# The odd mixer's input projection in seven block products instead of eight

## The reference, cut to what matters

```
def odd_mixer(h, cos, sin, cos_i, sin_i, w_in, w_out):
    qc, kc, vc, qi, ki, wi, qd, kd, vd = split_cols(h @ w_in, ODD_SPLITS)
    c_out = dsa_attention(partial_rope(qc...), partial_rope(kc...), vc, partial_rope(qi...), partial_rope(ki...), wi)
    d_out = moba_attention(partial_rope(qd...), partial_rope(kd...), vd)
    return jnp.concatenate([c_out, d_out], axis=-1) @ w_out
```

## Time and profile before

| | before |
|---|---|
| median of 3 runs | 3152.28 us (3148.3 to 3156.09) |
| the profiled execution, device time | 3152.17 us |
| its span in the trace | 3150.0 us |
| mean granted TensorE clock | 0.994 |
| TensorE matmuls busy | 3076.6 us (98%) |
| VectorE busy | 1917.6 us (61%) |
| ScalarE busy | 788.5 us (25%) |
| DMA, mean over the span | 211 GB/s |

### The profile page before, as it was taken

One profiled execution on the slowest core, in us unless ns is written; L12 is line 12 of the kernel. 1 busy time (PEld: TensorE's weight loads), 2 busy tenths in 40 slices (PEclk: granted clock), 3 DMA queues, 4 the chain that ended last, 5 costly groups with the idle time before them and its releaser, 6 DMA issues. The chain is left out here.

```text
span 3150.0 us, 46742 instructions
## 1 busy us (share of the span) xinstructions
PE 3076.6 (98%) x18521; PEld 1797.1 (57%) x18521; DVE 1917.6 (61%) x3306; ACT 788.5 (25%) x2066; POOL 162.0 (5%) x145
## 2 busy tenths in 40 slices
PE   9999999999999999999999899999999999999998
PEld 7845686784468567775685576864433333333333
DVE  7743786775477545623575546442377776677776
ACT  4412453351245243222252234230200000000000
POOL 0000000000000002310000104110100000000000
PEclk9999999999999999999999999999999999999999
DMA  7542045354424440123444421133699999999993
GB/s 292 189 179 107 33 182 209 125 187 156 167 88 178 169 182 27 67 93 137 175 177 184 154 98 66 55 141 124 259 402 420 418 419 420 366 414 418 419 417 137
DMA packets 81046, 665.52 MB, mean 211 GB/s; under 512 B 10528, under 2 KB 11168, under 8 KB 14016
## 3 DMA queue, kind: packets, MB, share of 16 engines
q1 hardware_dynamic: 78816, 655.41, 52.7%
q10 hardware_dynamic: 2016, 7.13, 0.6%
HBM read 661.46 MB, written 1.05 MB: 210 GB/s over the span
## 5 line engine op out<-in xcount | busy, mean ns | idle before, releaser
L4231 PE MATMUL psum<-ring,arena 128*32 128x512 f32 x5376 | 582.3, 592 | 0.0
L4231 PEld LDWEIGHTS psum<-ring,arena 128*32 128x32 f32 x5376 | 178.5, 110 | 397.6 <-issue 396.7
L887 PE MATMUL psum<-ring,arena 128*128 128x256 f32 x1760 | 398.1, 379 | 0.0
L887 PEld LDWEIGHTS psum<-ring,arena 128*128 128x128 f32 x1760 | 334.2, 190 | 46.1 <-issue 0.6
L887 PE MATMUL psum<-ring,xT_norm 128*128 128x256 f32 x1320 | 305.2, 381 | 1.4 <-DMA ring<-in_ffn_w 1.4
L940 ACT ACTIVATE arena<-arena 32x128 f32<-32x128 f32 x880 | 269.7, 306 | 31.4 <-DVE arena L1074 21.8
L999 DVE TENSOR_TENSOR ring<-ring 128x1024 f32<-128x1024 f32 x220 | 267.0, 1214 | 9.7 <-DMA ring<-in_ffn_w 3.3
L887 PEld LDWEIGHTS psum<-ring,xT_norm 128*128 128x128 f32 x1320 | 251.9, 191 | 36.3 <-DMA ring<-in_ffn_w 1.8
L4381 ACT ACTIVATE arena<-psum 128x256 f32<-128x256 f32 x84 | 32.5, 387 | 782.7 <-PE psum L4231 782.7
L907 PE MATMUL psum<-ring,arena 128*128 128x512 f32 x440 | 205.8, 592 | 0.0
L3091 PE MATMUL psum<-xT_norm,ring 128*128 128x256 f32 x832 | 184.8, 381 | 0.0
(11 more groups left out here) (636 smaller groups left out, 3884.5 us busy)
## 6 DMA issues: line engine op xcount, KB each, us to landing
ring<-in_moe_w SPq DMA_DIRECT2D x340, 1024.0 KB, 9.4
ring<-in_ffn_w SPq DMA_DIRECT2D x50, 2048.0 KB, 7.8
ring<-in_ffn_w SPq DMA_DIRECT2D x65, 1024.0 KB, 4.9
ring<-in_merge_w SPq DMA_DIRECT2D x16, 2048.0 KB, 8.3
ring<-in_feat_w SPq DMA_DIRECT2D x12, 2048.0 KB, 8.7
ring<-in_ev_in_w SPq DMA_DIRECT2D x4, 2048.0 KB, 8.9
ring<-in_od_in_w SPq DMA_DIRECT2D x4, 2048.0 KB, 9.6
ring<-in_merge_w SPq DMA_DIRECT2D x8, 1024.0 KB, 11.5
```

Source lines behind the costliest of these rows:

```text
L887: last = pe.matmul(psum[:, bank, 0:GROUP], a[:, k, :], w[:, k, :], start=(fresh and k == 0), stop=(k == KT // 2 - 1), skip_group_check=True)
L4231: last = pe.matmul(psum[part(j), r, :], xg[:, u.i, u.group // GROUPS, r * P + BLOCK * j:r * P + BLOCK * (j + 1)], m[:, j, :], start=(u.i = ...
```

## The change

The product of each chunk is done by Strassen's scheme in Winograd's form. The input is cut in 2 x 2 blocks (two row blocks, two halves of the features: 11, 12, 21, 22) and the chunk's weights too (two halves of the features, two halves of the columns). Seven block products of four matmuls each, 128 rows by half a chunk's columns, take the place of 2 x 8 matmuls over the whole chunk width. VectorE makes four differences or sums of weight blocks for each chunk (T1 to T4, 128 x 1024 each, `sum_on_vector`), four of input blocks once (S1 to S4, 128 x 512 each, `mix_on_vector`), and puts the block results together from the banks (`post`: u2, v, c22, c21, c12, and c11 in chunk 0). ScalarE copies P1 out of its bank (`copy_p1`) and scales each of the four blocks of a result (`settle`). Results are complete in the order c22, c11, c21, c12.

The order on VectorE is rewritten: posts and sums stand between the entry, the rotations and the picking of keys. The rotation of qd stands ahead of the posts of chunk 2; `pick_keys(0)` between the posts of chunks 2 and 3; the rotation of kd and `pick_keys(1)` between the posts of chunks 3 and 4; the rotation of qc behind all posts of chunk 4. P4 shares a PSUM bank with P6 and waits for `u2` of its own chunk, and P3 shares one with P5 and waits for `c22`. SyncE starts the later loads when a chunk's seven products are done. The filler matmuls no longer wait for ScalarE's last emptying.

```
+CHUNK_BANK = {"P1": 0, "P2": 0, "P6": 1, "P5": 2, "P3": 2, "P7": 3, "P4": 1}
+CHUNK_POSTED = (None, "u2", "v", "c22", "c21", "c12")
...
+    def posted_at(self, c, name):
+        return 1 if name == "c11" else 5 * c + 1 + CHUNK_POSTED.index(name)
...
+    def bank(self, c, name):
+        n, h = CHUNK_BANK[name], self.half(c)
+        if c == 0 and name == "P2":
+            n = 4
+        return self.prog.psum[:, n, 0:h]
...
+    def on_tensor(self, pe, c, name):
+        left, right = BLOCK_FACTORS[name]
+        if name == "P1":
+            self.weights.wait(pe, c)
+            if c == 1:
+                pe.wait_ge(self.posted, self.posted_at(0, "u2"))
+            if c:
+                pe.wait_ge(self.settled, 4 * (c - 1) + 2)
+        elif name == "P6" and c:
+            pe.wait_ge(self.posted, self.posted_at(c - 1, "c21"))
+        elif name == "P5" and c:
+            pe.wait_ge(self.posted, self.posted_at(c - 1, "c12"))
+        elif name == "P7" and c:
+            pe.wait_ge(self.posted, self.posted_at(c - 1, "v"))
+        elif name == "P4":
+            pe.wait_ge(self.posted, self.posted_at(c, "u2"))
+        elif name == "P2" and c:
+            pe.wait_ge(self.p1_copied, c + 1)
+        elif name == "P3":
+            pe.wait_ge(self.posted, self.posted_at(c, "c22"))
+        if left[0] == "S":
+            pe.wait_ge(self.mixed, {"S1": 1, "S2": 2, "S3": 3, "S4": 4}[left])
+        if right[0] == "T":
+            pe.wait_ge(self.summed, 4 * c + int(right[1]))
+        fresh = name != "P3" and not (name == "P2" and c)
+        a, w = self.x[left], self.factor(c, right)
+        for k in range(KT // 2):
+            last = pe.matmul(self.bank(c, name), a[:, k, :], w[:, k, :], start=(fresh and k == 0), stop=(k == KT // 2 - 1),
+                             skip_group_check=True)
+        last.then_inc(self.made, 1)
+    def copy_p1(self, act, c):
+        act.wait_ge(self.made, self.made_at(c, "P1"))
+        if c:
+            act.wait_ge(self.posted, self.posted_at(c - 1, "u2"))
+        act.activation(self.temps(c)[0][:, 0:self.half(c)], self.bank(c, "P1"), ACT.Copy).then_inc(self.p1_copied, 1)
+
+    def settle(self, act, c, name, func=ACT.Copy):
+
+        b, n = {"c22": (1, 1), "c11": (0, 0), "c21": (1, 0), "c12": (0, 1)}[name]
+        to = of = self.block(c, b, n)
+        if name == "c11" and c:
+            act.wait_ge(self.made, self.made_at(c, "P2"))
+            of = self.bank(c, "P1")
+        else:
+            act.wait_ge(self.posted, self.posted_at(c, name))
+        act.activation(to, of, func, scale=self.prog.rstd[:, b:b + 1]).then_inc(self.settled, 1)
+
+    def mix_on_vector(self, dve, i):
+        out, a, b, op = (("S1", "21", "22", ALU.add), ("S2", "S1", "11", ALU.subtract),
+                         ("S3", "11", "21", ALU.subtract), ("S4", "12", "S2", ALU.subtract))[i]
+        if i in (1, 3):
+            dve.wait_ge(self.mixed, i)
+        dve.tensor_tensor(self.x[out], self.x[a], self.x[b], op).then_inc(self.mixed, 1)
+
+    def sum_on_vector(self, dve, c, i):
+        out, a, b = (("T1", "12", "11"), ("T2", "22", "T1"), ("T3", "22", "12"), ("T4", "T2", "21"))[i]
+        if i == 0:
+            self.weights.wait(dve, c)
+        elif i in (1, 3):
+            dve.wait_ge(self.summed, 4 * c + i)
+        if c and i != 2:
+            dve.wait_ge(self.made, self.made_at(c - 1, ("P5", "P6", None, "P4")[i]))
+        dve.tensor_tensor(self.factor(c, out), self.factor(c, a), self.factor(c, b), ALU.subtract).then_inc(self.summed, 1)
...
+    def post(self, dve, c, name):
+
+        h = self.half(c)
+        p1, u2, v = (t[:, 0:h] for t in self.temps(c))
+        if name == "u2":
+            dve.wait_ge(self.made, self.made_at(c, "P6"))
+            dve.wait_ge(self.p1_copied, c + 1)
+            last = dve.tensor_tensor(u2, p1, self.bank(c, "P6"), ALU.add)
+        elif name == "v":
+            dve.wait_ge(self.made, self.made_at(c, "P7"))
+            dve.wait_ge(self.posted, self.posted_at(c, "u2"))
+            last = dve.tensor_tensor(v, self.bank(c, "P7"), u2, ALU.add)
+        elif name == "c22":
+            dve.wait_ge(self.made, self.made_at(c, "P5"))
+            dve.wait_ge(self.posted, self.posted_at(c, "v"))
+            last = dve.tensor_tensor(self.block(c, 1, 1), self.bank(c, "P5"), v, ALU.add)
+        elif name == "c11":
+            dve.wait_ge(self.made, self.made_at(c, "P2"))
+            dve.wait_ge(self.p1_copied, 1)
+            last = dve.tensor_tensor(self.block(c, 0, 0), self.bank(c, "P2"), p1, ALU.add)
+        elif name == "c21":
+            dve.wait_ge(self.made, self.made_at(c, "P4"))
+            last = dve.tensor_tensor(self.block(c, 1, 0), v, self.bank(c, "P4"), ALU.subtract)
+        else:
+            dve.wait_ge(self.made, self.made_at(c, "P3"))
+            last = dve.tensor_tensor(self.block(c, 0, 1), u2, self.bank(c, "P3"), ALU.add)
+        last.then_inc(self.posted, 1)
...
         @ph.block.sync
         def _(sp):
             for i in w_in.missing():
                 if i >= 4:
-                    sp.wait_ge(bank_full, TB * (i - 3))
+                    sp.wait_ge(blocks_of.made, 7 * (i - 3))
                 w_in.start(sp, i)
-            sp.wait_ge(bank_full, TB * 4)
+            sp.wait_ge(blocks_of.made, 7 * 4)
             w_out.start(sp, 1)
-            sp.wait_ge(bank_full, TB * 5)
+            sp.wait_ge(blocks_of.made, 7 * 5)
             w_out.start(sp, 0)
             for i in range(3):
...
             def chunk(c):
-                w_in.wait(pe, c)
-                n = ODD_CHUNKS[c]
-                w = w_in.buffer(c).rearrange("p (k n) -> p k n", k=KT)
-                for tb in range(TB):
-                    if c == 2:
-                        pe.wait_ge((z_ready, z_vector)[tb], 1)
-                    elif c > 2:
-                        pe.wait_ge(z_ready, 2 * (c - 2) + tb)
-                    for k in range(KT):
-                        if c == 0 and tb == 1 and k % 4 == 0:
-                            entry.wait_block(pe, (1, k // 4))
-                        last = pe.matmul(proj(c, tb), prog.xT[:, k, tb * P:(tb + 1) * P], w[:, k, :],
-                                         start=(k == 0), stop=(k == KT - 1))
-                    last.then_inc(bank_full, 1)
+                for name in blocks_of.order(c):
+                    blocks_of.on_tensor(pe, c, name)
...
-            pe.wait_ge(z_ready, 8)
-            stay_busy(prog, pe, 2, 4)
+            stay_busy(prog, pe, 3, 4)
...
             entry.on_scalar(act)
+            blocks_of.copy_p1(act, 0)
             act.wait_ge(entry.ready, 1)
-            empty(0, 0)
-            empty(1, 0)
-            empty(1, 1)
+            settle(0, "c22", "c11", "c21", "c12")
+            blocks_of.copy_p1(act, 1)
+            settle(1, "c22", "c11", "c21", "c12")
             fill(0)
-            empty(2, 0)
-            empty(2, 1)
+            blocks_of.copy_p1(act, 2)
+            settle(2, "c22", "c11", "c21")
             rectify(0)
             rectify(1)
-            empty(3, 0)
-            empty(3, 1)
-            empty(4, 0)
-            empty(4, 1)
+            settle(2, "c12")
+            blocks_of.copy_p1(act, 3)
+            settle(3, "c22", "c11", "c21", "c12")
+            blocks_of.copy_p1(act, 4)
+            settle(4, "c22", "c11", "c21", "c12")
             for f in (2, 4, 6):
...
-            entry.on_vector(dve)
-            entry.mean_on_vector(dve)
-            entry.invert_on_vector(dve)
-            dve.wait_ge(entry.ready, 1)
-            dve.wait_ge(bank_full, 2)
-            dve.tensor_scalar(z[:, 1, 0:starts[1]], proj(0, 1), prog.rstd[:, 1:2], None, ALU.mult).then_inc(z_vector, 1)
-            dve.wait_ge(z_ready, 1)
-            dve.wait_ge(z_vector, 1)
-            turn_angles(1, QI, NI, ID, 8, 4)
-            turn_angles(2, KI, 1, ID, 8, 4)
-            turn_angles(3, KC, 1, HD, 0, 8)
-            fill(1)
-            for b in range(TB):
+            def pick_keys(b):
...
-            for c, at in ((1, QD), (2, KD), (3, QC)):
-                dve.wait_ge(z_ready, 2 * c + 1)
-                turn_angles(3 + c, at, NH, HD, 0, 8)
+            def sums_behind(c, *which):
+                for i in which:
+                    blocks_of.sum_on_vector(dve, c, i)
+
+            post = lambda c, *names: [blocks_of.post(dve, c, name) for name in names]
+
+            blocks_of.sum_on_vector(dve, 0, 0)
+            entry.on_vector(dve)
+            dve.wait_ge(entry.copied, len(entry.blocks))
+            blocks_of.mix_on_vector(dve, 0)
+            blocks_of.sum_on_vector(dve, 0, 1)
+            blocks_of.mix_on_vector(dve, 1)
+            entry.mean_on_vector(dve)
+            blocks_of.mix_on_vector(dve, 2)
+            blocks_of.sum_on_vector(dve, 0, 2)
+            entry.invert_on_vector(dve)
+            blocks_of.sum_on_vector(dve, 0, 3)
+            blocks_of.mix_on_vector(dve, 3)
+            post(0, "c11", "u2")
+            sums_behind(1, 0, 1)
```

(82 more changed lines are left out.)

## The result

The changed kernel takes 3157.56 us (median of 22 runs, 3155.26 to 3163.22) against 3152.12 us (22 runs, 3148.3 to 3157.49): 5.4 us more. The ratio is 1.0014 with a 95% interval of 1.0009 to 1.002; it is taken over all runs and isn't the quotient of the two medians (1.0017), and by it the loss is 4.4 us, 2.8 to 6.3. That is slower, and clearly so, but by less than the 0.3% that the forecast took as the limit. Its profiled execution took 3156.61 us with a span of 3154.2, mean granted clock 0.993.

A forecast was written before the change was run, and what follows sets the result against it. TensorE was taken to set the pace, until VectorE has no slack from P4 of chunk 2. Chunk 0 +2.7, chunks 1 and 2 -1.5 and -1.7, then +6.4 to chunk 4's end, tail +0.8: +6.7, 3159.0 us, range 3154.5 to 3165.

The forecast's parts named there:

- a chunk of 512 columns by seven products: TensorE, chunks 1 to 4: 56 records of 256 columns take 12.08 us for 13.79, saving 1.71 us each.
- chunk 0 on TensorE: First chunk of the odd mixer: held back by VectorE's sums and posts, it ends 2.7 us later than before.
- VectorE's entry to the last mix: VectorE at the start of the odd mixer: copies, four sums, four mixes and small steps take 6.8 us.
- wait of P4 in chunk 4: TensorE in the last chunk: P4 waits 7.5 us for u2, which stands behind the second picking on VectorE.
- P4's start, from the entry's transposes: Last chunk: P4 starts when u2 is done at 848.9, forecast as 66.7 us after the entry's transposes.
- loss of clock in P4 and P3: Behind the wait in chunk 4: half clock for 4.5 us costs these two products 2.25 us.
- tail, more than before: After chunk 4: VectorE's c12 post, late rotation of qc and three copies add 0.8 us.
- stage, more than before: From the entry's transposes to the first attention matmul: 6.7 us longer, the whole forecast loss.
- first rival: Clock falls twice, also in chunk 0: end at 3161.3 us, above 3161.8 if it stays low longer; chance 0.27.
- VectorE's run: From P4 of chunk 2 on, 32 us without slack; rival: hand-overs lengthen some 35 steps, 3162 us, chance 0.08.
- The picking: Rival: second picking of keys hidden, so TensorE doesn't wait in chunk 4; 3149.2 us, chance 0.06.
- The estimate for a 584-wide sum: VectorE in chunk 0: each of four sums takes 0.75 us, against 1.2 for a 1024-wide one.

The follow-up runs named there:

- e5: Changed kernel with chunk 0 back to 16 plain matmuls, both banks emptied on ScalarE, without VectorE's sums and posts for it; 3155.8 us, 1.0009 of the kernel before.
- r_after_1: The changed kernel profiled again, nothing altered; whole time 3157.11 us, 77.89 us from the entry's transposes to the first attention matmul.
- r_after_2: A further profiled execution of the changed kernel, nothing altered; whole time 3157.62 us, 76.58 us from the entry's transposes to the first attention matmul.
- e1: Changed kernel with only the post u2 of chunk 4 put ahead of the second picking of keys on VectorE; 3157.2 us, 1.0014 of the kernel before.
- e4: Changed kernel with seven of the eight rounds of the second picking left out; 3148.5 us, 0.9986 of the kernel before.
- e3: Changed kernel with 30 filler matmuls put where TensorE waits in chunk 4, order kept; 3150.06 us, 0.9992 of the kernel before.
- e2: Changed kernel with the second picking cut up and chunk 4's posts set between its parts; 3156.27 us, 1.0013 of the kernel before.
- e6: Changed kernel with seven products for chunks 1 and 2 alone, chunks 0, 3 and 4 plain; 3147.79 us, 0.9985 of the kernel before.
- e7: Changed kernel with seven products for chunks 1 to 3, chunks 0 and 4 plain; 3148.11 us, 0.9992 of the kernel before.

## Why the prediction was right

The forecast was 3159.0 with 0.64 on a difference under 0.3%; 3157.56 came. Its steps, each as a difference within its own execution:

| step | forecast | measured |
|---|---|---|
| a chunk of 512 columns by seven products | 12.08 us | 12.09 |
| chunk 0 on TensorE | 10.7, loss 2.7 | 10.43, loss 2.4, or 2.6 against e5's 7.86 |
| VectorE's entry to the last mix | 6.8 | 6.7 (780.06 to 786.78) |
| wait of P4 in chunk 4 | 7.5 | 7.39 |
| P4's start, from the entry's transposes | 66.7 | 66.50 |
| loss of clock in P4 and P3 | 2.25 | 3.15; 2.99 in r_after_1, 1.70 in r_after_2 |
| tail, more than before | 0.8 | 4.97 - 4.06 = 0.9 |
| stage, more than before | 6.7 | 7.5 in the profile, 7.3 and 6.0 in the others |
| attention | 0 | -1.4, or 0 |

The mechanism was right in place, and in size but for the clock: e1 shows that the wait follows the posts, e4 that it is the picking's length, e5 that chunk 0 and the wait are separate costs, e3 that the clock is one of its own. The term that was mis-sized is the clock: 2.25 us forecast, 3.15, 2.99 and 1.70 measured. "Run at half clock for 4.5 us" rested on one stretch; here it was half until 852.8, 6.2 us of work. And the forecast let the attention phase alone, which came out 1.4 us shorter. The two errors have opposite signs: 6.7 + 0.8 - 1.4 = 6.1 us, which is the 106.56 - 100.52 = 6.0 of the profiles. That they cancel is luck, and a part of why the median came so near. The 0.7 us between 6.1 and the measured 5.4 is less than the runs scatter. The 0.33 for slower by over 0.3% was too much even by the prediction's own figures, since the main case of its first rival, 3161.3, lies under the limit of 3161.8.

The rival with the clock falling in chunk 0 did not come: no window between 780 and 842 has less than 1.00, with waits of 0.51 and 1.77 us in it. VectorE's run was not longer than its rows: from c21 of chunk 2 to the end of u2 of chunk 4 it took 31.8 us, 32.0 forecast. The picking was not hidden. The estimate for a 584-wide sum, 0.75, was 0.76; P1 and P2 of chunk 0 take 782.95 - 780.96 = 1.99 us for 16 records, 0.124 each, in proportion to the columns (0.216 x 146 / 256 = 0.123), so the weight loads, 0.192 us each and overlapped, don't set the pace at 146 columns. The Trainium skill ("TensorE: Matmul & The Clock Gate", Back-to-back issue gap) has the spacing of matmuls set by the weight load too; by it these records would be slower than their columns say, and the trace shows nothing of it.

What was not forecast lies outside the two phases. e3 is 7.5 us under the changed kernel and its stage explains 3.1. The rest is in one place of a later phase. TensorE's timeline of the changed kernel there, then that of e3, each from the same pair of records to the next pair that both have:

```profile
1367.23 0.70 PE L2525 MATMUL psum<-ring,xT_norm 128*128 128x256 f32 x2
...
1371.41 0.18 PE L2602 MATMUL psum<-arena,ring 32*32 32x32 f32 x1 [2.42 <-issue]
...
1371.61 2.08 PE L2525 MATMUL psum<-ring,xT_norm 128*128 128x256 f32 x4
...
1381.10 1.08 PE L2540 MATMUL psum<-ring,xT_norm 128*128 128x512 f32 x2
```

```profile
1365.16 0.70 PE L2529 MATMUL psum<-ring,xT_norm 128*128 128x256 f32 x2
...
1366.92 1.13 PE L2529 MATMUL psum<-ring,xT_norm 128*128 128x256 f32 x4
...
1374.88 1.08 PE L2544 MATMUL psum<-ring,xT_norm 128*128 128x512 f32 x2
```

The windows there, the changed kernel first (behind the wait), e3 second:

```profile
1372.00:1373.00 1.00, 1.00 (x3) 0.78 (x3) 0.97 (x2) 0.29 (x1) 0.00 (x0) 0.50 0.99 418
```

```profile
1367.00:1372.00 5.00, 5.00 (x71) 4.17 (x72) 1.80 (x3) 1.18 (x2) 0.00 (x0) 1.00 0.98 411
```

In the changed kernel TensorE stands still for 2.42 us, and "issue" says that the profile shows nothing it waits for; behind that the granted clock is 0.50. In e3 there is neither. The stretch takes 1381.10 - 1367.23 = 13.87 us against 1374.88 - 1365.16 = 9.72, so 4.15 us, and 3.07 + 4.15 = 7.2 of the 7.5 are found.

This is not chance from run to run. The wait, 2.18 to 3.04 us long, is in all three executions of the kernel before and all three of the changed one, and in e1, e2, e4 and e5. In the six of the ten that have the changed kernel's TensorE program it stands ahead of the same matmul record, in the three of the kernel before each time ahead of another. In e3, e6 and e7, whose TensorE programs have another length, it is missing, and the stretch takes 9.72, 9.72 and 10.08 us (13.67 to 15.70 in the kernel before). These three have one trace each, and e5, also of another length, has the wait. So it goes with TensorE's program and not with VectorE's order (e1, e2 and e4 change that alone); what the engine waits for isn't known. 3.6 to 4.2 us of the time that e3, e6 and e7 gain is this and not the edit's own work, which is why the stage, and not the whole time, was compared from run to run.

## What to carry to other kernels

Before a product is traded for vector work, write the vector engine's order out from the first step without slack and add up to the next result that TensorE needs; the engine's share of the whole span (62%) says nothing on it. Where a long serial block on VectorE stands in the way, cutting it up around the posts gave back 3.9 us of the stage (e2) and was still 3.6 us short of no change; stopping the scheme short of it gave more: three chunks of five gained 4.2 us in the stage where all five lost 7.5. A wait of TensorE costs its length and the clock behind it; filler matmuls in it gave 3.1 us back. And a whole time that moves by a few us should be traced to its place: here 4 us came and went with a wait 500 us further on.

## What the runs showed of the hardware

Behind the same wait of 7.39 us, the same kernel lost 3.15 us to the lower clock in one execution and 1.70 in another, and where it lost less, the attention phase behind it was longer by 1.38 (29.87 for 28.49). The two phases together were steady within 0.2 us in these three executions, each alone was not. A forecast by one row of a clock's recovery was good to about a us here, no better.

TensorE can stand still for 2.2 to 3.0 us with nothing in the profile that it waits for, at the same record in every execution of one TensorE program (six executions of one, three of another), and not in the one trace each of three kernels whose TensorE program is a little longer or shorter (e3, e6, e7).
